# Mixing a layer's two branches: order of its units, of the last gate unit and of the splits ahead of it

## The reference

```python
    proj = h @ w_in
    mqk, mv, mo, mi, mf, aq, ak, av, ga, gb = jnp.split(proj, offsets, axis=-1)
    ...
    hm = (hm.reshape(B, S, M_V_WIDTH) * jax.nn.sigmoid(mo.astype(jnp.float32))).astype(h.dtype)
    ha = sliding_window_attention(...)
    y = jax.nn.sigmoid(ga) * (hm @ w_branch_m) + jax.nn.sigmoid(gb) * (ha @ w_branch_a)
    return y @ w_out
```

## Time and profile before

| | |
|---|---|
| median of 3 runs | 2229.71 us (2229.05 to 2230.18) |
| profiled execution: its time | 2229.75 us |
| profiled execution: its span | 2228.0 us |
| granted TensorE clock | 0.996 |
| TensorE matmuls busy | 98% |
| VectorE, ScalarE, POOL busy | 47%, 49%, 44% |

### The profile page before, as it was taken

The page is one execution under the profiler, slowest core; times in us unless marked ns, Lnnn a source line. Parts: engine busy times, 40 slices in busy tenths (PEclk is TensorE's granted clock), DMA queues, the critical chain, the costliest instruction groups (busy, mean ns, idle before and its releaser), DMA issues.

```text
span 2228.0 us, 31566 instructions
## 1 busy us (share of the span) xinstructions
PE 2178.1 (98%) x10287; PEld 1793.3 (80%) x10287; DVE 1046.1 (47%) x2195; ACT 1085.3 (49%) x2273; POOL 971.9 (44%) x757
## 2 busy tenths in 40 slices
PE   7999999999999999999999999999999999999997
PEld 5888888788888888888888788888888787777766
DVE  7365364523231234563563623321324726767773
ACT  5466466434232234464564624322324427787783
POOL 3333333444444444434333344544544334555544
PEclk9999999999999999999999999999999999999999
DMA  3222222223322322222322223323322431211213
GB/s 131 85 86 67 94 78 69 82 94 107 101 95 94 104 94 95 85 76 76 95 70 83 67 94 110 99 95 97 102 94 94 155 123 58 74 64 53 76 32 121
DMA packets 60288, 198.70 MB, mean 89 GB/s; under 512 B 6815, under 2 KB 13520, under 8 KB 59537
## 3 DMA queue, kind: packets, MB, share of 16 engines
q1 hardware_dynamic: 53808, 183.77, 25.2%
q10 hardware_dynamic: 6368, 13.50, 1.7%
HBM read 192.99 MB, written 4.26 MB: 89 GB/s over the span
## 4 chain that ended last, share of the span: by engine, by line
issue 57%; POOL 26%; PE 9%; DVE 5%; ACT 1%; POOLq 1%; DMA 0%; DVEq 0%; SPq 0%; ACTq 0%
POOL w_lo L541 26%; PE ps L639 2%; PE ps L641 2%; PE ps L640 2%; DVE Pn L2183 1%; PE ps L976 1%; PE ps L967 1%; PE ps L989 1%; DVE PTn L2199 1%; POOLq L537 1%; PE ps L990 1%; POOLq L539 1%; DMA w_raw<-w_all 0%; DVE y L2170 0%; DVE ocur L2212 0%
## 5 line engine op out<-in xcount | busy, mean ns | idle before, releaser
L541 POOL TENSOR_TENSOR w_lo<-w_raw,w_hi 128x512 fp32r<-128x512 f32 x592 | 778.4, 1322 | 1065.9 <-ACT w_hi L1056 1064.2
L639 PE MATMUL ps<-hT_hi,w_hi 128*128 128x512 f32 x1600 | 643.4, 402 | 1.9 <-DVE hT_lo L1732 1.3
L641 PE MATMUL ps<-hT_hi,w_lo 128*128 128x512 f32 x1600 | 626.0, 391 | 0.0
L640 PE MATMUL ps<-hT_lo,w_hi 128*128 128x512 f32 x1600 | 624.9, 391 | 0.0
L1056 ACT ACTIVATE w_hi<-w_raw 128x512 fp32r<-128x512 f32 x664 | 410.8, 626 | 414.1 <-PE ps L641 380.2
L641 PEld LDWEIGHTS ps<-hT_hi,w_lo 128*128 128x128 f32 x1600 | 301.0, 188 | 65.3
L639 PEld LDWEIGHTS ps<-hT_hi,w_hi 128*128 128x128 f32 x1600 | 301.5, 188 | 62.1 <-issue 2.4
L640 PEld LDWEIGHTS ps<-hT_lo,w_hi 128*128 128x128 f32 x1600 | 301.9, 189 | 57.6 <-issue 0.5
L639 PE MATMUL ps<-u_hi,w_hi 128*128 128x512 f32 x512 | 199.2, 389 | 0.0
L640 PE MATMUL ps<-u_lo,w_hi 128*128 128x512 f32 x512 | 199.2, 389 | 0.0
L641 PE MATMUL ps<-u_hi,w_lo 128*128 128x512 f32 x512 | 199.2, 389 | 0.0
(11 more groups left out here) (330 smaller groups left out, 3437.9 us busy)
## 6 DMA issues: line engine op xcount, KB each, us to landing
w_raw<-w_all SPq DMA_DIRECT2D x332, 512.0 KB, 3.3
bias<-scr_w ACTq DMA_DIRECT2D x8, 512.0 KB, 3.7
biasn<-scr_n SPq DMA_DIRECT2D x4, 1024.0 KB, 5.2
w1k<-w_in ACTq DMA_DIRECT2D x2, 1024.0 KB, 7.4
w1v<-w_in ACTq DMA_DIRECT2D x1, 2048.0 KB, 12.8
scr_x<-x ACTq DMA_DIRECT2D x1, 2048.0 KB, 7.5
x<-scr_x SPq DMA_DIRECT2D x1, 2048.0 KB, 9.2
out<-x SPq DMA_DIRECT2D x16, 128.0 KB, 1.8
```

The lines of the kernel that those rows point to most:

```text
L541: nc.gpsimd.tensor_tensor(w_lo[:, h, :], raw[:, h // 2, (h % 2) * HALF:(h % 2 + 1) * HALF], w_hi[:, h, :].bitcast(F32), ALU.subtract).then ...
L639: nc.tensor.matmul(ps[:, p, :], wh, hi[:, kk, :], start=(kk == 0), stop=False)
L640: nc.tensor.matmul(ps[:, p, :], wh, lo[:, kk, :], start=False, stop=False)
L641: last = nc.tensor.matmul(ps[:, p, :], wl, hi[:, kk, :], start=False, stop=(kk == KT - 1))
```

## The change

`WINDOW_END` becomes an order like that of `WINDOW_NEXT`, with one quarter fewer ahead of `wsa 0` and one fewer ahead of `WT 0,0`. At its end the first four `hm` parts stand ahead of the last quarter, the products `WV 3,*` behind it, and `wsum 2` and `wsum 3` last, behind all `hm` parts. The readout of the last gate unit (gb 1) moves from its last quarter to behind the last `hm` part, on ScalarE and on VectorE; the copy of the next weight half stays at the quarter. `MIX` becomes three quarters of pm 0, one of pm 1, the last of pm 0, three of pm 1, then pa 0 and pa 1; the weights lie in memory in the order pm, pm, pa, pa. ScalarE's high parts of `ha` move from ahead of the mixing into its first turn, behind the copy of the first half of pa 0's weights. VectorE waits for each low part of y.

```diff
-WINDOW_END = (WINDOW[:WINDOW.index(("wsum", 2)) + 1] + [("mc", k) for k in range(4)]
-              + [("WV", 3, 1), F, ("mc", 4), ("mc", 5), ("TH", 1), ("mc", 6), ("mc", 7), ("wsum", 3)])
+WINDOW_END = [F, ('hnorm', 0), F, ('WS', 0, 0), ('WS', 0, 1), F, ('vlo',), ('WS', 1, 0), ('WS', 1, 1), ('wrec', 0), F, ('wsa', 0), ('wrec', 1), F, ('WT', 0, 0), ('wsa', 1), ('WS', 2, 0), ('hnorm', 1), ('WS', 2, 1), ('hnorm', 2), F, F, ('wrec', 2), F, ('WT', 1, 0), F, ('WT', 1, 1), F, ('WV', 0, 0), ('wsa', 2), F, ('WS', 3, 0), ('WS', 3, 1), ('TH', 0), F, ('wrec', 3), ('wsum', 0), F, ('WT', 2, 0), ('WV', 1, 0), ('WT', 2, 1), ('wsa', 3), ('WV', 1, 1), F, F, ('wsum', 1), ('WT', 3, 0), ('WT', 3, 1), ('WV', 2, 0), ('WV', 2, 1), ('mc', 0), ('mc', 1), ('mc', 2), ('mc', 3), F, ('TH', 1), ('mc', 4), ('mc', 5), ('WV', 3, 0), ('WV', 3, 1), ('mc', 6), ('mc', 7), ('wsum', 2), ('wsum', 3)]
...
-MIX = unit("pm", 0) + unit("pa", 0) + unit("pm", 1) + unit("pa", 1)
+LAST_GATE = ("u1", "gb", 1)
+MIX = unit("pm", 0)[:3] + unit("pm", 1)[:1] + unit("pm", 0)[3:] + unit("pm", 1)[1:] + unit("pa", 0) + unit("pa", 1)
...
+                        if s == LAST_GATE and it == NG - 1:
+                            last_gate = cur["u"]
+                            split(last_gate.n + 2, last_gate.m + 1, last_gate.b, 1)
...
                             nc.scalar.activation(hm_hl[0][:, s[1], :], hm32[:, s[1], :], ACT.Copy).then_inc(mhi, 1)
+                            if s[1] == KT - 1:
+                                store(LAST_GATE, last_gate)
...
+                def split_ha():
+                    for f in free:
+                        act.wait_ge(*f)
+                    ha_tiles = ha32[:, :, :, :].rearrange("p g n s -> p (g n) s")
+                    for k in range(KT):
+                        nc.scalar.activation(ha_hl[0][:, k, :], ha_tiles[:, k, :], ACT.Copy).then_inc(mhi, 1)
...
+                        gemm_step(s, cur[s[1:]])
+                        if first and s == ("h0", "pm", 0):
+                            split_ha()
...
                     V.tensor_tensor(y_hl[1][:, cur["i2"] + n, :], t3[:, n, :], y_hl[0][:, cur["i2"] + n, :].bitcast(F32),
                                     ALU.subtract).then_inc(y_done, 1)
+                    dve.wait_ge(y_done, cur["ny"] + n + 1)
...
-        per_unit += [np.stack([pm, pa], 1).reshape(-1, P, KT * P), _units(inp["w_out"][l])]
+        per_unit += [np.concatenate([w.reshape(4, 2, P, KT * P) for w in (pm, pa)], 1).reshape(-1, P, KT * P), _units(inp["w_out"][l])]
```

More of the change, by code:

```diff
@@ L819, in _ @@
                         if s[0] == "u0":
-                            cur["u"] = us[0]
+                            cur[s[1:]] = us[0]
                         second = s[1] == "pa"
-                        quarter(s, cur["u"], *(ha_hl if second else hm_hl),
+                        quarter(s, cur[s[1:]], *(ha_hl if second else hm_hl),
                                   waits=(lambda k: (mlo, l * 2 * KT + second * KT + k + 1)) if s[2] == 0 else None)
@@ L1294, in turn @@
                         us = take(s)
-                        if s[0] in UNIT_STEPS:
+                        if s == LAST_GATE and it == NG - 1:
+                            last_gate = cur["u"]
+                            split(last_gate.n + 2, last_gate.m + 1, last_gate.b, 1)
+                        elif s[0] in UNIT_STEPS:
                             gemm_step(s, cur["u"])
@@ L1374, in _, with mix_turn @@
                     turn(it, steps)
[L1375 to L1382, removed]
+                free = [(g_free[b_], w.next("u", b_) + 1) for b_ in range(2)] + [(t_free[b_], w.next("T", b_) + 1) for b_ in range(2)] \
+                    + [(o_free[b_], w.next(f"O{b_}") + 1) for b_ in range(2)]
+                def split_ha():
[4 more added lines that the diff above has]
+                        nc.scalar.activation(ha_hl[0][:, k, :], ha_tiles[:, k, :], ACT.Copy).then_inc(mhi, 1)
+                def mix_turn(i, first):
                     cur["ny"], cur["i2"] = l * KT + i * 2, i * 2
@@ L1385, in _ @@
                         take(s)
-                        gemm_step(s, cur["u"])
+                        gemm_step(s, cur[s[1:]])
+                        if first and s == ("h0", "pm", 0):
+                            split_ha()
+                mix_turn(0, True)
+                with w.loop(act, 3, per(MIX)) as i:
+                    mix_turn(i + 1, False)
                 ln_exp()
@@ L1875, in turn @@
                         us = take(s)
-                        if s[0] == "u1":
+                        if s == LAST_GATE and it == NG - 1:
+                            last_gate = cur["u"]
+                        elif s[0] == "u1":
                             store(s, cur["u"])
@@ L1999, in _ @@
                         if s[0] == "u1":
-                            store(s, cur["u"])
+                            store(s, cur[s[1:]])
                 for i in range(4):
```

## The result

The changed kernel takes 2234.09 us (median of 10 runs, 2228.24 to 2237.51) against 2229.97 us (10 runs, 2228.96 to 2232.47): a ratio of 1.0017, 95% interval 1.0009 to 1.0025. It is 0.17% slower: a small difference, but its interval does not contain 1, and no change was forecast. The time lies inside the range that was given. Its runs also spread over 9 us, those of before over 3.5 us.

The account below looks back on a forecast made before the run. TensorE, busy 98%, was taken as the bound: its matmul starts and the idle time before them. Its waits would move from `ha` to pm0's bank, layer 1 0.2 us later, layer 2 0.1 to 0.3 earlier: 2229.7 us, range 2225.9 to 2234.5.

Parts of the forecast that it names:

- The window: Last head turn: TensorE stalls 1.7 us at `WT 0,0` for ScalarE; mixing still starts 0.2 us earlier, at 394.9.
- VectorE's chain to pm0's bank: VectorE empties pm0 only behind `ha`'s low parts, so pa0 starts at 409.2 after a 3.1 us TensorE wait.
- Its eight quarters with pa1, 10.88: Mixing behind pa0's start: pa0 and pa1 take 10.88 us, so the second turn starts at 420.1.
- POOL's collisions: VectorE's low parts: POOL costs the fifth `hm` part 0.3 us and holds `ha`'s first part to 403.5.
- Rival 3: POOL holds VectorE's `hm` and `ha` low parts more often, 2.4 us per layer: 2234.5 us; chance 0.18.
- Each late microsecond first eats the 3.1 us wait at pa0, and costs nothing: If bank 1, taken early by pm1, is freed late, the 3.1 us wait at pa0 absorbs it.
- The sum: Both layers together: between -0.2 and +0.2 us, taken as 0, giving 2229.7 us.
- Rival 1: Mixing: pm0's bank is free by 406.1, TensorE gains 2.8 and 3.1 us: 2223.8 us; chance 0.12.

Follow-up runs that it names:

- again: The changed kernel run once more unaltered, for its trace; 2232.67 us (one run).
- oldwin: The changed kernel with the old `WINDOW_END` list put back, crossed mixing order kept; 2229.03 us, ratio 1.0001.
- early: The changed kernel with VectorE's product of pm0 in the first mixing turn ahead of `ha`'s eight low parts; 2221.48 us, ratio 0.9971.
- earlysplit: "earlywin" with ScalarE's copy of pa0's second weight half behind the fourth of `ha`'s high parts, not the eighth; 2221.52 us, ratio 0.9967.
- uncross: The changed kernel with the old mixing order (pm0, pa0, pm1, pa1) and weights in that order; 2235.04 us, ratio 1.0023.
- earlywin: "early" with one quarter moved in the last window to stand ahead of `WT 0,0`; 2220.64 us, ratio 0.9961.
- earlylate: "early" with ScalarE's copy of pa0's first weight half behind `ha`'s eight high parts instead of ahead; 2229.74 us, ratio 1.0005.
- earlyold: "early" with the window list of the kernel before; 2225.84 us, ratio 0.9987.

## Why the prediction was wrong

- **The window.** Right in kind: TensorE stands at `WT 0,0` for ScalarE's scaling. 1.7 us were forecast; the first two transposes went ahead and 1.03 us of idle time were left behind them. The mixing starts at 64.5 behind the marker, forecast 64.8.
- **VectorE's chain to pm0's bank.** Right in each step to 0.4 us, up to `ha`'s eighth part: `hm`'s parts start at 63.4 (forecast 63.6), the sigmoid ends at 69.7 (69.9), ScalarE's first part of `ha` starts at 72.4 (72.5), the first low part at 73.1 (73.4), pa0 at 79.1 in layer 2 (79.1). The wait there was 2.99 us, forecast 3.1.
- **"Its eight quarters with pa1, 10.88".** This is the step that failed. The 10.88 us are from a stretch in which TensorE had been busy; behind 3 to 4 us of idle time they took 12.5 and 12.6. The forecast priced this stretch at full clock and gave the long wait in front of it no price of its own. In "again", where the clock stayed in layer 1, the second turn started at 90.04, and 90.0 had been forecast.
- **POOL's collisions.** One was sized at 0.3 us, and came (the four `hm` parts took 2.94 for 2.5). One at the eighth part of `ha`, behind pa0's second weight half, was put at nothing: it cost VectorE 1.05 us in layer 1, and in layer 2 and in "again" it fell on POOL. The prediction's own figures had it: POOL done at 408.8, so started at about 407.4, and the eighth part at 403.5 + 7 x 0.62 = 407.8. Rival 3 had the mechanism and a wrong place for it. That its 2234.5 is so near the measured time is luck: it was made of 4.8 us of holds by POOL, of which 1.05 us came, and not of the clock.
- **"Each late microsecond first eats the 3.1 us wait at pa0, and costs nothing"** was said of pm1's bank. In the changed kernel that bank held nobody. In "oldwin" it held TensorE 0.92 us, the wait at pa0 was 1.16 us, and the clock stayed: lateness there costs nothing, and may even keep the clock.
- **The sum.** 1.65 + 1.7 for the clock and 1.05 for the collision are 4.4 us over the forecast; the difference of the medians was 4.1. Both are matters of chance by execution, which fits the wide spread of the runs. The ten runs bear the clock's share out. The 76 runs of the kernel before average 2231.7 us where the clock was 0.994 and 2227.0 where it was 0.997, or 1.6 us for each 0.001. The changed kernel's clock is 0.0018 lower, which makes an estimated 2.9 us.
- **Rival 1** (the gain of the crossing) was given 2223.8. With one instruction moved it was there, at 2221.5, so what it needed was not a chain 3.1 us shorter but another order of the same chain.

The stretches outside the changed ones differ between executions too: the marker of layer 1 lies at 327.4 to 330.9 in the traces, and from layer 2's second mixing turn to the end of the span it is 948.6 to 953.8 us. The clock goes with this as well. In that last stretch the traces of "early", "oldwin" and "earlysplit" have no low clock until shortly before the span ends, and take 948.6 to 949.0 us; that of "before" has one such place and takes 950.7, that of "uncross" has four and takes 953.8. "early" and "earlywin" gain 2.4 and 2.7 us more in their medians than the markers show. Their clocks, 0.9967 and 0.9964 against 0.9956, make an estimated 1.7 and 1.2 us of that by the 1.6 us above.

What stays open is what decides whether the clock falls behind a given wait, whether the higher clock of "early" outside the mixing is more than chance, and where the last microsecond of its gain comes from.

## What to carry to other kernels

Reordering matmuls on the busiest engine asks for PSUM banks in another order; look first at where in the emptying engine's queue the instruction stands that frees the bank now asked for earliest, and move it. A weight copy and a bank that were hidden behind one wait come due together when it goes. Here the crossing alone, the crossing with the copy ahead ("oldwin") and, under the new window, the crossing with the product ahead ("earlylate") each left the time where it was. All three together took 3.5 us off under the old window ("earlyold") and 7.8 under the new one ("early"). And TensorE's idle time isn't to be priced at its length: waits of 2.5 to 4 us here could cost another 1.6 us behind them, and one in "uncross" some 3.

## What the runs showed of the hardware

- Of 13 waits of TensorE at pa0 with over 2 us of idle time, 7 had slow matmuls (1.2 GHz) behind them: those of 4.02, 3.34, 3.31, 3.00, 2.99, 2.95 and 2.47 us. Six had none: 3.00, 2.98, 2.95, 2.94, 2.07 and 2.03 us. The same wait in the same kernel went either way (2.99 in the changed kernel and 2.95 in "again"). None of 1.58 us or less at this place had any. With slow matmuls pa0 and pa1 took 12.5 to 12.6 us in place of 10.9 to 11.05. In "uncross" the low clock lasted longer in layer 1 than in layer 2: from pa0 to the second turn 19.26 us at 0.84 and 17.74 us at 0.92.
- The clock also fell where TensorE had no idle time at all. In "again" it was 0.50 from 912.6 on; in the 7 us ahead the records leave no gap and the clock was 1.00; 16 small matmuls (L713) are the last of them:

```profile
910.54 1.94 PE L713 MATMUL ps<-ident,grow 4*128 4x4 f32 x16
...
905.00:912.50 7.50, 7.50 (x46) 6.23 (x44) 6.78 (x8) 4.70 (x10) 3.05 (x3) 1.00 0.41 137
912.60:916.00 3.40, 3.40 (x9) 2.64 (x9) 2.19 (x9) 2.32 (x4) 0.00 (x0) 0.50 0.42 150
```

- Twelve matmuls that nobody reads, put into such a wait, kept the clock in both layers of the trace, and over 11 runs it averaged 0.9960, against 0.9938 without them.
- Where a low part of `hm` or `ha` on VectorE and POOL's `w_lo` meet, one of them is held. In the 14 traces it goes by how far VectorE's record starts behind POOL's. At 0.01 to 0.09 us (6 cases) VectorE took its usual 0.69 us and POOL was held: 1.82 to 1.92 us instead of 1.3. At 0.36 to 0.51 us (18 cases) VectorE was held: 1597 to 1787 ns. At 0.20 to 0.23 us it went either way: VectorE was held in 6 cases of 17, POOL in 11. In the changed kernel 0.22 and 0.23 us fell on different sides, and that decided over 1.05 us. The Trainium skill ("SBUF — State Buffer", "SBUF: two separate sides") says that whichever starts first has the port for its whole instruction. This trace agrees that one of the two is held, but by the recorded starts POOL was first in both layers and was the one held in layer 2, so a lead of 0.2 us in the profile doesn't tell who has the port.
